# Two buffers for the recurrent gates of branch B, and two gate chunks moved ahead of the first sample's value pages

## What is computed

```python
h = x * (1.0 + scale[:, None]) + shift[:, None]
aq, af, ai, az, bx, bz, cq, ckv, cg, cz, mg = jnp.split(h @ w_in, splits, axis=-1)
...
def rglru_branch(xb, z, conv0, h0, conv_w, conv_b, ga_w, ga_b, gx_w, gx_b, lam):
    xpad = jnp.concatenate([conv0.astype(xb.dtype), xb], axis=1)
    u = conv_b + sum(xpad[:, j:j + T] * conv_w[j] for j in range(CONV_W))
    ub = u.reshape(B, T, B_BLOCKS, B_BW)
    r = jax.nn.sigmoid(jnp.einsum('btnd,nde->btne', ub, ga_w).reshape(B, T, W) + ga_b)
    ig = jax.nn.sigmoid(jnp.einsum('btnd,nde->btne', ub, gx_w).reshape(B, T, W) + gx_b)
    log_a = -LRU_C * r * jax.nn.softplus(-lam)
    a = jnp.exp(log_a)
    bterm = jnp.sqrt(-jnp.expm1(2.0 * log_a)) * (ig * u)
    bterm = bterm.at[:, 0].add(a[:, 0] * h0)
    _, hs = lax.associative_scan(_lin_combine, (a, bterm), axis=1)
    y = hs * jax.nn.silu(z)
    return y, hs[:, -1], xpad[:, T:]
...
branch = jnp.einsum('btnc,ncd->btnd', ys, w_branch)
merged = jnp.sum(jax.nn.sigmoid(mg).reshape(B, T, N_BRANCH, D) * branch, axis=2)
x_new = layer_norm(ALPHA * x + gate[:, None] * (merged @ w_out), ln_g, ln_b)
```

## Time and profile before

| | us |
|---|---|
| median of three runs | 1803.81 |
| lowest, highest | 1794.69, 1806.71 |
| the profiled execution | 1793.93 |
| its span, first to last instruction | 1792.1 |
| mean granted TensorE clock in it | 0.968 |

### The profile page before, as it was taken

One profiled execution on the slowest core, in us unless ns is written; L12 is line 12 of the kernel. 1 busy time (PEld: TensorE's weight loads), 2 busy tenths in 40 slices (PEclk: granted clock), 3 DMA queues, 4 the chain that ended last, 5 costly groups with the idle time before them and its releaser, 6 DMA issues. The chain is left out here.

```text
span 1792.1 us, 30521 instructions
## 1 busy us (share of the span) xinstructions
PE 1612.0 (90%) x11996; PEld 1418.2 (79%) x11996; DVE 901.9 (50%) x1431; ACT 562.7 (31%) x1111; POOL 473.8 (26%) x461
## 2 busy tenths in 40 slices
PE   7899988988896799999989998989899986999997
PEld 3788975666665688888869998888799976899997
DVE  1651366666661222332223358857873373557577
ACT  0312135545451323222211233626352466000100
POOL 2012101000002112111131357657663122135500
PEclk9899999999998899999999999989999998999999
DMA  9321120000004444434223301202032110544422
GB/s 303 125 60 49 25 84 1 1 1 1 1 2 109 111 113 123 115 107 126 75 93 121 119 25 36 68 29 73 25 97 74 26 50 25 171 143 149 167 84 83
DMA packets 162433, 142.89 MB, mean 80 GB/s; under 512 B 50902, under 2 KB 152306, under 8 KB 161522
## 3 DMA queue, kind: packets, MB, share of 16 engines
q1 hardware_dynamic: 153298, 127.20, 23.5%
q10 hardware_dynamic: 8992, 13.74, 2.2%
HBM read 115.62 MB, written 29.40 MB: 81 GB/s over the span
## 5 line engine op out<-in xcount | busy, mean ns | idle before, releaser
L1016 PE MATMUL ps<-w_hi,h_hi 128*128 128x256 f32 x792 | 228.5, 289 | 5.9 <-DVEq L151 2.9
L1016 PE MATMUL ps<-w_lo,h_hi 128*128 128x256 f32 x792 | 223.7, 282 | 0.0
L1016 PE MATMUL ps<-w_hi,h_lo 128*128 128x256 f32 x792 | 223.6, 282 | 0.0
L1016 PE MATMUL ps<-h_hi,w_hi 128*128 128x344 f32 x600 | 199.1, 332 | 3.1 <-ACT ak L1960 1.4
L1016 PE MATMUL ps<-h_lo,w_hi 128*128 128x344 f32 x600 | 193.2, 322 | 0.0
L1016 PE MATMUL ps<-h_hi,w_lo 128*128 128x344 f32 x600 | 192.7, 321 | 0.0
L1016 PE MATMUL ps<-h_hi,wg_hi 128*128 128x344 f32 x432 | 146.3, 339 | 14.2 <-ACT gate_stage L1806 13.3
L1016 PEld LDWEIGHTS ps<-w_hi,h_hi 128*128 128x128 f32 x792 | 150.9, 191 | 8.0 <-DVEq L151 3.3
L1016 PEld LDWEIGHTS ps<-w_hi,h_lo 128*128 128x128 f32 x792 | 150.8, 190 | 0.0
L1016 PEld LDWEIGHTS ps<-w_lo,h_hi 128*128 128x128 f32 x792 | 150.8, 190 | 0.0
L907 POOL CAST w_hi<-w_raw 128x1024 fp32r<-128x1024 f32 (+1 forms) x48 | 52.5, 1094 | 356.2 <-DMA w_raw<-in_w_in 165.9
(11 more groups left out here) (446 smaller groups left out, 3623.4 us busy)
## 6 DMA issues: line engine op xcount, KB each, us to landing
w_raw<-in_w_in SPq DMA_DIRECT2D x46, 512.0 KB, 4.9
sgm<-gate_spill SPq DMA_DIRECT2D x22, 516.0 KB, 6.2
gate_spill<-gate_stage ACTq DMA_DIRECT2D x54, 172.0 KB, 2.4
w_raw<-in_w_in SPq DMA_DIRECT2D x34, 256.0 KB, 4.4
adw<-in_ada_w SPq DMA_DIRECT2D x8, 1024.0 KB, 11.3
pgc<-in_cache_nsa_kv SPq DMA_DIRECT2D x128, 64.0 KB, 2.4
pg<-in_cache_nsa_kv SPq DMA_DIRECT2D x64, 128.0 KB
w_raw<-in_w_branch SPq DMA_DIRECT2D x12, 512.0 KB, 5.2
```

What stands on the lines that cost most here:

```text
L1016: last = mm(out, lhsT=l, rhs=r, start=(first and i == 0 and j == 0), stop=(final and i == n - 1 and j == 2), skip_group_check=joint)
```

## The change

Branch B gets two buffers each for BR and BI (the even BR lies at O_CS, where SGM 0 comes later; the place of the old BA product is taken by BZ itself, which now holds the output y). ScalarE's waits change with it: for BXP on `u_ready` instead of `b_done`; the sigmoids of block jj on `b_done(jj - 1)` instead of `b_done(jj)`; a new wait on `b_scan(jj)` ahead of the exponentials; waits on `b_done(3)` before SGM 0 and on `b_done(j - 1)` before BZ. VectorE copies the BXP columns into OCO, now with four buffers, at the start of the convolution and the BHS columns right after the scan. In the sample stage a place ("start", 2) with two chunks stands on TensorE between `hidden(0)` and the transposes of groups 4 to 6, on ScalarE behind `tap_b(0)`; samples 1 and 3 have six chunks instead of seven. The number of instructions is the same.

```diff
--- before.py
+++ after.py
@@ -194,8 +194,8 @@
 def gate_chunks():
 
     plan, n = {}, 0
-    for key, count in ([(("start", 0), 2), (("start", 1), 2)]
-                       + [((b, i), 1) for b in range(NS) for i in ((2, 3, 4, 6, 7) if b == NS - 1 else (1, 2, 3, 4, 6, 7, 8) if b % 2 else (2, 3, 4, 6, 7, 8))]):
+    for key, count in ([(("start", 0), 2), (("start", 1), 2), (("start", 2), 2)]
+                       + [((b, i), 1) for b in range(NS) for i in ((2, 3, 4, 6, 7) if b == NS - 1 else (1, 2, 3, 4, 6, 7, 8) if b == 5 else (2, 3, 4, 6, 7, 8))]):
         plan[key] = range(n, n + count)
         n += count
     assert n == GCH
@@ -460,13 +460,13 @@
     BXP = sb("bxp", o_, [2, 8 + 3 + T]); o_ += 2 * 1040
     BZ = sb("bz", o_, [2, TC]); o_ += 2 * TC
     BU = sb("bu", o_, [2, TC]); o_ += 2 * TC
-    BR = sb("br", o_, [TC]); o_ += TC
-    BI = sb("bi", o_, [TC]); o_ += TC
+    BR = [sb("br_even", O_CS, [TC]), sb("br_odd", o_, [TC])]; o_ += TC
+    BI = [sb("bi%d" % i, o_ + TC * i, [TC]) for i in range(2)]; o_ += 2 * TC
     BA = sb("ba", o_, [TC]); o_ += TC
     BT = sb("bt", o_, [TC]); o_ += TC
     BHS = sb("bhs", o_, [TC]); o_ += TC
     GWB = sb("gwb", o_, [2, 2, P]); o_ += 512
-    OCO = sb("oco", o_, [2, 32]); o_ += 64
+    OCO = sb("oco", o_, [4, 32]); o_ += 128
     OCR = sb("ocr", o_, [4, P], parts=32); o_ += 512
     assert o_ <= END, o_ - END
 
@@ -1334,6 +1334,7 @@
         page_transposes(0, range(4))
         pe.wait_ge(ld["w1"], (6 + 4) * 16)
         hidden(0)
+        gates("start", 2)
         page_transposes(0, range(4, 7))
         hidden_sum(0)
         for b in range(NS):
@@ -1571,7 +1572,7 @@
         def columns_out(j):
 
             pe.wait_ge(e("oc_cols"), j + 1)
-            nc.tensor.transpose(ps[0:20, 6, P * j:P * j + P], OCO[:, j % 2, 0:20], ID).then_inc(e("oc_rows"), 1)
+            nc.tensor.transpose(ps[0:20, 6, P * j:P * j + P], OCO[:, j, 0:20], ID).then_inc(e("oc_rows"), 1)
 
         for j in range(5):
             if j < 4:
@@ -2002,7 +2004,7 @@
                         if j == 0:
                             act.wait_ge(e("a_free"), 4)
                         if j >= 2:
-                            act.wait_ge(e("b_done"), j - 1)
+                            act.wait_ge(e("u_ready"), j - 1)
 
                         st(A(BXP[:, j % 2, 0:8], ps[:, b, 0:8], CP))
                         st(A(BXP[:, j % 2, 11:3 + CH], ps[:, b, 8:CH], CP), act3.free)
@@ -2011,18 +2013,21 @@
                 st.mark(e("bx_ready"))
             if j:
                 jj = j - 1
-                if jj:
-                    act.wait_ge(e("b_done"), jj)
-                for x, dst in ((0, BR), (1, BI)):
+                gr = BR[jj % 2]
+                if jj >= 2:
+                    act.wait_ge(e("b_done"), jj - 1)
+                for x, dst in ((0, gr), (1, BI[jj % 2])):
                     for c in range(3):
                         b = ta.take(act)
                         st(A(dst[:, CH * c:CH * c + CH], ps[:, 3 + b, 0:CH], ACT.Sigmoid, bias=PRM[:, 48 + 4 * x + jj:49 + 4 * x + jj]), ta.free)
 
-                st(A(BA, BR, ACT.Exp, scale=C8[:, jj:jj + 1]))
-                st(A(BT, BR, ACT.Tanh, scale=C8[:, 4 + jj:5 + jj]))
-
-                st(A(BR, BT, ACT.Ln, bias=1.0))
-                st(A(BR, BR, ACT.Exp, scale=-1.0), e("b_at"))
+                if jj:
+                    act.wait_ge(e("b_scan"), jj)
+                st(A(BA, gr, ACT.Exp, scale=C8[:, jj:jj + 1]))
+                st(A(BT, gr, ACT.Tanh, scale=C8[:, 4 + jj:5 + jj]))
+
+                st(A(gr, BT, ACT.Ln, bias=1.0))
+                st(A(gr, gr, ACT.Exp, scale=-1.0), e("b_at"))
 
             def b_gate(x):
                 for c in range(3):
@@ -2030,15 +2035,18 @@
                     st(A(SGM[x][:, CH * c:CH * c + CH], ps[:, b, 0:CH], ACT.Tanh, scale=0.5), act3.free)
 
             if j == 4:
+                act.wait_ge(e("b_done"), 3)
                 b_gate(0)
             if j < 4:
+                if j >= 2:
+                    act.wait_ge(e("b_done"), j - 1)
                 for c in range(3):
                     b = act3.take(act)
                     st(A(BZ[:, j % 2, CH * c:CH * c + CH], ps[:, b, 0:CH], CP), act3.free)
             if j:
                 act.wait_ge(e("b_om"), jj + 1)
                 st(A(BT, BT, ACT.Sqrt, scale=2.0))
-                st(A(BR, BZ[:, jj % 2, :], ACT.Sigmoid), e("b_sq"))
+                st(A(gr, BZ[:, jj % 2, :], ACT.Sigmoid), e("b_sq"))
             if j == 4:
                 b_gate(1)
 
@@ -2482,6 +2490,8 @@
             cb = PRM[:, 44 + j:45 + j]
             v.wait_ge(e("bx_ready"), j + 1)
             xp, us, up = BXP[:, s, 8:11 + T], BU[:, s, 0:NS], BU[:, s, NS:TC]
+            st(cp(OCO[:, j, 0:8], BXP[:, s, 0:8]))
+            st(cp(OCO[:, j, 8:11], BXP[:, s, 8 + T:11 + T]))
             st(ts(up, xp[:, 0:T], cw[0], cb, MUL, ADD))
             for i in (1, 2, 3):
                 st(stt(up, in0=xp[:, i:i + T], scalar=cw[i], in1=up, op0=MUL, op1=ADD))
@@ -2498,23 +2508,21 @@
             s = j % 2
             v.wait_ge(e("b_at"), j + 1)
 
-            st(tt(BT, BT, BR, MUL), e("b_om"))
-            st(tt(BI, BI, BU[:, s], MUL))
+            gr, gi, y = BR[s], BI[s], BZ[:, s]
+            st(tt(BT, BT, gr, MUL), e("b_om"))
+            st(tt(gi, gi, BU[:, s], MUL))
             st(tt(BHS[:, 0:NS], BA[:, 0:NS], CST[:, j, 24:32], MUL))
             v.wait_ge(e("b_sq"), j + 1)
-            st(tt(BI, BI, BT, MUL))
-            st(tt(BHS[:, 0:NS], BHS[:, 0:NS], BI[:, 0:NS], ADD))
-            st(V.tensor_tensor_scan(BHS[:, NS:TC], BA[:, NS:TC], BI[:, NS:TC], 0.0, MUL, ADD))
-            st(tt(BZ[:, s], BZ[:, s], BR, MUL))
-            st(tt(BA, BHS, BZ[:, s], MUL))
-            st(cp(YH[0][:, j], BA))
-            st(tt(YH[1][:, j], BA, YH[0][:, j].bitcast(F32), SUB))
-
-            oc = OCO[:, s]
-            st(cp(oc[:, 0:8], BXP[:, s, 0:8]))
-            st(cp(oc[:, 8:11], BXP[:, s, 8 + T:11 + T]))
+            st(tt(gi, gi, BT, MUL))
+            st(tt(BHS[:, 0:NS], BHS[:, 0:NS], gi[:, 0:NS], ADD))
+            st(V.tensor_tensor_scan(BHS[:, NS:TC], BA[:, NS:TC], gi[:, NS:TC], 0.0, MUL, ADD), e("b_scan"))
+            oc = OCO[:, j]
             st(cp(oc[:, 11:12], BHS[:, TC - 1:TC]))
             st(cp(oc[:, 12:20], BHS[:, 0:8]))
+            st(tt(y, y, gr, MUL))
+            st(tt(y, BHS, y, MUL))
+            st(cp(YH[0][:, j], y))
+            st(tt(YH[1][:, j], y, YH[0][:, j].bitcast(F32), SUB))
             if j:
                 b_rows(j - 1)
             st.mark(e("oc_cols"))
```

## The result

The changed kernel takes 1772.94 us (median of 4 runs, 1768.32 to 1779.49), the kernel before beside it 1803.48 (4 runs, 1794.69 to 1806.71). The ratio is 0.9849, with a 95% interval of 0.9821 to 0.9877: faster, by 30.5 us between the medians.

The account below looks back on a forecast made before the run. TensorE, busy 90% of the span, was taken as the bound, so only less idling or fewer half-rate matmuls help. Branch B's 20.1 us plus the sample stage's 7.2 give 27.3, median 1776.5 us, range 1765.7 to 1790.

Parts of the forecast that it names:

- First stall: Branch B: TensorE's 3.60 us wait between gate halves goes, second half runs faster; less a 0.8 weights wait, gain 4.3.
- Second stall: Branch B, next block: the 3.92 us wait between gate halves goes, matmuls behind it run faster; gain 4.5 us.
- Third stall: Branch B, last block: ScalarE's 11.57 us idle before the sigmoids goes, 0.6 returns as scan wait; gain 11.0 us.
- From the last exponentials on: Branch B, last sigmoids to first merge matmul: nothing rearranged, the recurrence's shorter end saves 0.3 us.
- `b_done(3)` ahead of SGM 0 costs nothing: Branch B: `b_done(3)` comes 5 us behind the scan, the exponentials take 8 us, so the new wait is free.
- Rival (2): Branch B: GpSimd's splits hold the scan back 5.6 us, giving 1782.1 us; chance 0.11.
- The sample stage: Two gate chunks hidden in a value-page wait, samples 1 and 3 shortened 8.2 us; less later page waits, gain 7.2.
- The spare 1.5 us: Sample stage: two chunks take 8.3 us of TensorE's 9.80 us wait for the first value pages, leaving 1.5.
- (1): Sample stage: page loads set the pace, the removed chunk becomes page wait, no gain there; 1783.7 us, chance 0.12.
- (3): Branch B, last block: ScalarE's idle moves behind the second buffer; only 16.3 us gained, 1787.5 us, chance 0.10.
- (4): Whole kernel: TensorE's granted clock falls when kept denser, making it slower, over 1822 us; chance 0.02.
- From profile to median: Whole kernel: profiled 1793.93 us becomes 1766.6; the median, 9.9 above the profiled execution, becomes 1776.5, -1.5%.

Follow-up runs that it names:

- after: The changed kernel's first profile, with no further edit; the profiled execution took 1768.32 us.
- after_again: The changed kernel as it is, run a second time beside a later variant; 1771.52 us, ratio 0.9834 to the kernel before.
- weights_early: Changed kernel, but SyncE's queue takes the last projection's weights ahead of the gate weights and the wait for the first recurrence; 1769.37 us.
- gates_late: Changed kernel, but ScalarE's sigmoids of block jj wait again for the whole recurrence jj-1, as with single BR and BI; 1787.04 us.
- three_chunks: Changed kernel with a third gate chunk ahead of the first sample's value pages, taken from sample 5; 1769.83 us.
- split_late: Changed kernel, but GpSimd holds the splits of the first two merge weights until the third scan is done; 1776.97 us.
- sample_only: Kernel before with only the sample part of the change, the new gate chunk plan; 1793.34 us, ratio 0.995 to the kernel before.
- short_samples: Changed kernel, but the two early chunks are taken from samples 2 and 4, which had six, instead of 1 and 3; 1777.05 us.

## Why the prediction was right

It was right in its result and its mechanism, and in the profile of after its two sums came out too, 19.6 for 20.1 and 6.9 for 7.2. Part of that is luck: several terms were off and in part they offset each other, and the 6.9 is the largest of eight profiles, whose mean is 5.2.

**First stall, forecast 4.3, measured 3.4.** The wait went and the twelve products run at 3.63 us in one row, as forecast. The mis-sized term is the wait for weights behind it: forecast 0.8, measured 1.79, and up to 3.0 in `after_again`. I moved GpSimd's split by 0.4 us and left its duration at 2.40; in the new place its last subtraction lies under VectorE's product and takes 3.21. `weights_early` took the wait away.

**Second stall, forecast 4.5, measured 4.2.** Right, with no new wait behind it.

**Third stall, forecast 11.0, measured 10.4.** The idle time of 11.57 is gone and what remains is the wait for the scan. I gave that as 0.6, and it is 2.47. Two things make up the difference. The sigmoids end 8.69 us after the last eviction of BZ instead of the 9.98 that I worked out, since the last six gate products run in 2.01 us instead of 3.52 and the sigmoids follow them without gaps; that makes the wait longer and costs nothing. The scan ends 11.08 after that eviction instead of 10.54, as its product takes 3.24 us, not the 2.69 of the earlier trace rows. Only this half microsecond is a loss. `gates_late` confirms that the buffers and not something else carry the stall.

**From the last exponentials on, forecast 0.3, measured 1.7.** The shorter end of the recurrence is 0.3: from product to merge 10.11 us against 10.41. The rest I had called "nothing is rearranged". But ScalarE's eviction of the third SGM part had waited 1.38 us for TensorE; that product now is done when ScalarE comes, since TensorE got further ahead. It is a gain that I missed, and by chance it fills what the scan and the weights took. It hangs on the 2.01 us of the last six gate products: in `three_chunks`, where they took 2.99, ScalarE waited 0.76 us at this eviction, and from the last exponentials to the merge it took 25.5 us instead of 24.9.

**`b_done(3)` ahead of SGM 0 costs nothing.** Right: the evictions at 1490.49 have no idle before them. `split_late` showed how near it is: three stretched operations put a wait of 2.26 us there.

**Rival (2), GpSimd's splits over the scan.** The splits did come to lie there, and one of three operations was caught, as I chose; not three. The end that I kept in the range was no fiction: in `split_late` three operations of one recurrence took 8.1 us instead of 3.2. The Trainium skill, page "SBUF — State Buffer", section "Who interferes with whom", calls the shared port pair an exclusive lock, held for the whole instruction by whichever starts first. The traces agree: the stretched product ended 1.09 us after the subtraction's end in the earlier trace rows, after and `split_late` alike.

**The sample stage, forecast 7.2, measured 6.9, 4.0 and 4.0** (after, `sample_only`, `after_again`); over the eight profiles with this plan and the old loads the mean is 371.4 against 376.55, a gain of 5.2. The two chunks are hidden, as forecast: the wait of 9.80 is gone (the 1.5 us that I had left of it are 0 in after, 1.56 in `sample_only` and 2.89 in `weights_early`), and sample 0's last chunk is at 637.96 against 637.63. Samples 1 and 3 fell from 44.91 and 45.41 to 40.99 and 41.34. The spare 1.5 us did not come through: the waits for the pages behind grew from 3.2 to 4.7 and from 3.0 to 3.7. The mis-sized term is what SyncE's weight load costs sample 2, whose pages stand behind it. I gave that 0.8 us, from the one row of 8.10 in the earlier trace rows. In after the wait grew by 0.5 (0.31 to 0.85), in `after_again` by 2.2, and the interval of sample 2 by 0.5 and 3.4 (41.55 and 44.45 against 41.08). The place was right and the size too small as a middle.

**Rivals (1), (3), (4).** (1) holds for five chunks, not for six (`short_samples`). (3) fell: of the 11.57 us only 2.47 moved to the scan. (4) fell: the stretch from the merge on took 259.6 instead of 258.6 us at a clock of 0.97 instead of 0.98. That 1 us is no effect of the change: the fourteen profiles have 258.6 to 259.7 there, seven of those with the new branch B under 258.8.

**From profile to median.** The profiled time was forecast at 1766.6 and came at 1768.32, a gain of 25.6 us for the 27.3 of the sum. The median was forecast at 1776.5 and is 1772.94: before had its median 9.9 above its profiled execution, after only 4.6. That is the scatter of a few runs, and no part of the mechanism; that the median's gain, 30.5 us, lies above the sum and the profile's below it says nothing about the terms.

## What to carry to other kernels

A buffer that lets one engine run a block ahead pays by the stall minus whatever is late next, so follow the releases past the removed wait until one is later than the old work; here that was a scan 0.5 us behind the estimate and weights 1 us behind it. When work moves in time, check which operations of the engine that shares memory ports with it now lie over it: moving the splits off one recurrence operation merely put them over three others. Where two releases lie within some 2 us, taking the later one away pays only up to the other, and two profiles of a kernel can differ in which is later; so compare a variant with a profile that has the same waits and clock ahead of the edit. Work that fills a wait is worth moving only out of places where TensorE and not the loads set the pace, and a profile shows them: a wait for pages of some 0.3 us at six chunks meant that a seventh could go and a sixth could not.

## What the runs showed of the hardware

**VectorE and GpSimd block each other in turn.** A 1032-column VectorE product of 1.23 us that began under a GpSimd subtraction ended 1.1 us after it each time, so it took from 1.46 us (`gates_late`) to 3.32 (`split_late`), by how much of the subtraction was left. GpSimd pays as well: its subtraction of 2.35 to 2.40 us took 3.21 to 3.47 when it began beside a product. In `split_late` an instruction with one input was caught too: VectorE's cast, 0.70 us elsewhere, took 1.42 between two operations of GpSimd. The profile of before already had such a one, the convolution's first operation (L2485), 3.11 us instead of 0.81: it began at 1382.58 under a subtraction that ended at 1384.68. I had reckoned with instructions of two inputs alone, and with one side losing.

**Filling a wait raised the clock at once.** From 577 to 587 us TensorE was busy 0.20 us at a granted clock of 0.70 before, and 8.95 us at 1.00 after. In the stretch behind it, 593 to 640 us, it was the other way round: 0.93 before, 0.85 after, with 1.8 us less of busy time, and that sample's end did not move.
